# Experts loop of a hybrid decoder step: transpose of the first activation half placed before the last up grain, first tail down block placed after the first down grain, some lo splits placed later

## What is computed

```python
gu   = xs @ w_gu[e] + b_gu[e]                  # 1024 -> 2048
gate = minimum(gu[:, :1024], 7.0)
up   = clip(gu[:, 1024:], -7.0, 7.0)
act  = gate * sigmoid(1.702 * gate) * (up + 1.0)
out  = (act @ w_down[e] + b_down[e]) * prob    # 1024 -> 1024
y    = segment_sum(out, token)
```

## Time and profile before

| | us |
|---|---|
| median of 3 runs (lowest, highest) | 2195.52 (2192.89, 2197.51) |
| profiled execution, span | 2192.6 |
| PE busy in it | 2059.1 (94%) |
| DVE busy | 1621.2 (74%) |
| ACT busy | 1279.9 (58%) |
| POOL busy | 784.6 (36%) |
| start of the first item, end of the last | 665.90, about 2142.7 |

### The profile page before, as it was taken

The page is one execution under the profiler, slowest core; times in us unless marked ns, Lnnn a source line. Parts: engine busy times, 40 slices in busy tenths (PEclk is TensorE's granted clock), DMA queues, the critical chain, the costliest instruction groups (busy, mean ns, idle before and its releaser), DMA issues.

```text
span 2192.6 us, 38702 instructions
## 1 busy us (share of the span) xinstructions
PE 2059.1 (94%) x11946; PEld 1503.0 (69%) x11947; DVE 1621.2 (74%) x2213; ACT 1279.9 (58%) x1717; POOL 784.6 (36%) x997
## 2 busy tenths in 40 slices
PE   6998999999958999999999999999999999999995
PEld 4996766666647676676666677767676676777552
DVE  4533456666668687787777689988897798899667
ACT  3632443334316676676765568767776676877544
POOL 3224345555623233223331323433232233334124
PEclk7999999999969999999999999999999999999997
DMA  9767511211268787898887789999898898999665
GB/s 343 232 222 267 170 49 51 68 49 54 87 229 330 264 316 281 293 351 289 278 310 255 260 294 375 364 341 331 290 370 324 287 339 333 345 359 390 243 226 180
DMA packets 154530, 572.25 MB, mean 261 GB/s; under 512 B 22560, under 2 KB 41773, under 8 KB 120165
## 3 DMA queue, kind: packets, MB, share of 16 engines
q1 hardware_dynamic: 127405, 511.87, 62.1%
q0 software_dynamic: 25520, 56.53, 10.6%
q10 hardware_dynamic: 1552, 3.13, 0.4%
HBM read 521.36 MB, written 50.29 MB: 261 GB/s over the span
## 4 chain that ended last, share of the span: by engine, by line
PE 53%; DVE 6%; issue 6%; ACT 4%; DVEq 1%; DMA 0%; ACTq 0%; POOLq 0%
PE pg L2235 9%; PE pg L2236 9%; PE pg L2238 9%; PE py L2194 6%; PE py L2170 4%; PE py L2171 4%; PE py L2174 4%; PE pg L2208 3%; DVE lo L2459 3%; ACT hi L2371 2%; PE pt L2165 1%; PE pg L2228 1%; DVE pair L2477 1%; DVE pair L2473 1%; ACT sigm L2379 1%
## 5 line engine op out<-in xcount | busy, mean ns | idle before, releaser
L2235 PE MATMUL pg<-hi,xs 128*128 128x512 f32 x1056 | 429.4, 407 | 0.0
L2236 PE MATMUL pg<-lo,xs 128*128 128x512 f32 x1056 | 411.8, 390 | 0.0
L2459 DVE TENSOR_TENSOR lo<-spare,hi 128x1024 fp32r<-128x1024 f32 x264 | 306.3, 1221 | 85.2 <-ACT hi L2371 82.2
L2459 DVE TENSOR_TENSOR lo<-w_out,hi 128x1024 fp32r<-128x1024 f32 x272 | 312.4, 1220 | 59.2 <-ACT hi L2371 59.1
L2238 PE MATMUL pg<-hi,xs 128*128 128x512 f32 x1056 | 325.5, 389 | 0.0
L2459 DVE TENSOR_TENSOR lo<-raw,hi 128x1024 fp32r<-128x1024 f32 x264 | 314.1, 1220 | 7.1
L2371 ACT ACTIVATE hi<-spare 128x1024 fp32r<-128x1024 f32 x264 | 260.2, 1050 | 43.7 <-PE pg L2238 43.7
L2371 ACT ACTIVATE hi<-raw 128x1024 fp32r<-128x1024 f32 x264 | 271.0, 1053 | 25.1 <-PE pg L2238 24.2
L2371 ACT ACTIVATE hi<-w_out 128x1024 fp32r<-128x1024 f32 x272 | 265.5, 1050 | 32.4 <-SPq L2002 28.0
L2235 PEld LDWEIGHTS pg<-hi,xs 128*128 128x128 f32 x1056 | 198.3, 188 | 72.7 <-DVE lo L2459 13.3
L2170 PE MATMUL py<-hi,aT 128*128 128x512 f32 x528 | 218.8, 414 | 12.1 <-ACT aT L2383 5.5
(11 more groups left out here) (487 smaller groups left out, 3646.2 us busy)
## 6 DMA issues: line engine op xcount, KB each, us to landing
w_out<-in_w_gu SPq DMA_DIRECT2D x136, 1024.0 KB, 6.9
spare<-in_w_gu SPq DMA_DIRECT2D x132, 1024.0 KB, 10.3
raw<-in_w_down SPq DMA_DIRECT2D x132, 1024.0 KB
ada_w<-in_w_ada SPq DMA_DIRECT2D x4, 2048.0 KB
spare<-in_w_ada SPq DMA_DIRECT2D x4, 2048.0 KB
moe_rows<-small SPq DMA_DIRECT2D x9, 512.0 KB, 6.7
w_v<-in_w_in SPq DMA_DIRECT2D x2, 2048.0 KB, 17.4
w_i<-in_w_in SPq DMA_DIRECT2D x2, 2048.0 KB, 18.6
```

The lines of the kernel that those rows point to most:

```text
L2235: pe.matmul(pg[u][b][:, :], xs[:, kt, 0, :], wh[:, u, :], start=False, stop=False)
L2236: pe.matmul(pg[u][b][:, :], xs[:, kt, 0, :], wl[:, u, :], start=False, stop=False)
L2459: dve.tensor_tensor(lo[q % RING][:, :, :], grain(q % GRAINS), hi[q % RING][:, :, :].bitcast(F32), ALU.subtract).then_inc(s["lo"], 1)
```

## The change

On PE, `transpose_act(i, 0)` moves from behind up grain 15 to in front of it. `down_tail(i, 0, tail)` moves from in front of down grain 0 to behind it. On DVE, the order of the lo splits around the two activations is another: `head` ends with grain 17, not 18; splits 18 and 19 stand behind `swiglu(i, 0)`; split 20 stands between `rows_lo` of half 0 and `act_lo` of half 1; split 21 between `act_lo` of half 1 and `rows_lo` of half 1; splits 22 and 23 behind that, and `select` last. No instruction is added or removed, and the orders of ACT, SP and POOL are as they were.

```diff
@@ tensor engine, item(i, tail)
                 for q in range(HEAD, GU):
+                    if q == GU - 1:
+                        transpose_act(i, 0)
                     if tail and q in TAILED:
                         pe.wait_ge(s["lo"], i * GRAINS + q + 1)
...
                     up_grain(i, q)
 
-                transpose_act(i, 0)
                 if tail:
                     tail_act(i, tail)
                 transpose_rows(i + 1, 0)
...
-                    if tail and kt == 0:
+                    if tail and kt == 1:
                         pe.wait_ge(s["aT_t"], i + 1)
                         down_tail(i, 0, tail)
                     down_grain(i, kt)
@@ vector engine
             def head(i):
-                for q in range(RING, GU + 3):
+                for q in range(RING, GU + 2):
                     split_lo(i, q)
...
             def foot(i):
                 swiglu(i, 0)
-                for q in range(GU + 3, GU + 5):
+                for q in range(GU + 2, GU + 4):
                     split_lo(i, q)
                 act_lo(i, 0)
                 swiglu(i, 1)
                 rows_lo(i + 1, 0)
+                split_lo(i, GU + 4)
+                act_lo(i, 1)
                 split_lo(i, GU + 5)
-                split_lo(i, GU + 6)
-                act_lo(i, 1)
                 rows_lo(i + 1, 1)
+                for q in range(GU + 6, GU + 8):
+                    split_lo(i, q)
                 select(i + 1)
-                split_lo(i, GU + 7)
                 for q in range(RING):
                     split_lo(i, GRAINS + q)
```

## The result

The changed kernel is slower. It takes 2271.7 us in the median of four runs (2270.82 to 2272.34), the kernel before 2194.2 us (2192.3 to 2197.51): ratio 1.0357, 95% interval 1.0345 to 1.037. The forecast was 2170, with 2165 to 2181 as range.

What follows compares the result with a forecast made beforehand. PE, busy 94%, and a nearly even DVE in items without tails bound the kernel. Gains of 7.2, 10.3, 8.2 and 0 make 25.7 us; 2195.5 less that gives 2169.8, range 2165 to 2181.

Steps and rivals of the forecast that it cites:

- the term for the back-to-back items: Eight items without a tail behind another such: DVE loses idle times of 0.67 and 0.26 us, 0.9 gained each, 7.2 total.
- The rival on the other side: DVE's unbroken splits delay POOL's copy of the row weights by 2.5 us in 17 items: 2213 us, chance 0.04.
- The early transpose: Half 0's transpose on PE, ahead of up grain 15: same 0.44 us cost, waits 1.5 us at most behind tails.
- The tail's first block: The tail's down block on PE, behind down grain 0: net 0.68 us gained per item with a tail of 32.
- Tail of 64: Four items: the early transpose's wait of 0.63 and 0.1 for switches take back 0.78; nothing, within 0.2 us.
- DVE's two checks: In DVE's new order, half 1's lo part and the next rows' second half keep 0.4 and 0.3 us to spare.
- The period of 35.9 set by DVE: Back-to-back items without a tail: DVE's own work of 35.9 us is the floor of their length.
- The sum: Gains over all items without a tail and with tails of 32 and 64: 25.7 us off in all.
- 8.86: Time in us from the start of the first activation on DVE to the transpose of half 1 on PE.
- DMA as the floor: Weights can't come faster in back-to-back items, so their 7.2 us gain goes: 2177 us, chance 0.07.
- DVE's new waits: Both reserves in DVE's order fail, DVE stands about 0.6 us in each of 17 items: 2180 us, chance 0.12.
- No effect: Something unseen sets the period and the change doesn't reach the bound: 2195 us stays, chance 0.04.

Runs made afterwards that it cites:

- e3: The changed kernel plus one DVE clamp of about 0.6 us, its only input in PSUM, ahead of the split of grain 8: 2228.6 us, ratio 1.0164.
- e4: The changed kernel plus one DVE subtraction of about 0.6 us, two inputs in SBUF, ahead of the split of grain 8: 2279.3 us, ratio 1.0396.
- e5: The changed kernel, with DVE waiting once for its own last split ahead of the split of grain 8, no instruction added: 2168.4 us, ratio 0.9876.
- e7: The changed kernel plus a small DVE instruction reading 32 columns of PSUM ahead of each of splits 8, 10 and 12: 2171.9 us, ratio 0.9895.
- e9: The changed kernel with one DVE wait ahead of split 8, and half 0's transpose left behind grain 15 for tails of 64: 2166.2 us, ratio 0.9869.
- e6_small_psum: The changed kernel plus one small DVE instruction reading 32 columns of PSUM ahead of the split of grain 8: 2219.3 us, ratio 1.0113.

## Why the prediction was wrong

**The step that failed** is the term for the back-to-back items, 8 x 0.9 = 7.2, and in it the sentence "I take that DVE loses both its idle times". DVE did lose the 0.67 us, but the prediction put nothing against it, with "SP's and POOL's lists are untouched" as its ground. That idle time was not waste: it was the opening through which POOL's scatter and gather got their turn. In 8 items its loss cost 11.8 us each where 0.9 was to be gained. `e3` against `e4` shows that DVE's kind of instruction decides, `e5` and `e7` that the opening takes back the whole of the loss. Not all of the 11.8 is time held off: in the mean of the eight the scatter's instruction ends 12.3 us later in the item than before, its landing takes 5.1 us longer, and 6 us had been to spare.

**The rival on the other side** was the right mechanism at the wrong instruction. It named DVE's unbroken splits, POOL and the missing 0.67, with 0.04 as its chance and 2213 as its time. But it looked at the copy of `now`, which is indeed held off and indeed harmless, and not at the scatter ahead of it in POOL's list. Its price of 2.5 us in 17 items stood on no row; the runs show 11.8 in 8. The scatter was held off in the same item already (4.40 us, where one that gets through at once takes 1.6 to 1.75), and what it delays is the rest of DVE's run and then a landing of 10 us. I never asked of each POOL instruction what it would do if DVE had no gap, though DVE's run without a gap was itself part of the forecast.

**Point by point, most of the rest held.** The early transpose costs nothing by itself and waits behind tails, 1.25 us (1.5 at the most had been forecast); the item is 37.72 all the same. The tail's first block: an item with a tail of 32 got 0.58 shorter (49.08 to 48.50); 0.68 had been counted. Tail of 64: 0.06 longer, forecast as nothing; the early transpose waits there as forecast, and `e9` takes it back. DVE's two checks held: PE doesn't wait before down grain 6, apart from the stall late in the first two items, which the kernel before had as well (3.6 and 2.9 us; now 3.7 and 4.8). The period of 35.9 set by DVE: 35.8 in `e5`. The sum: 25.7 us off; `e5_self_wait`, the same change with an opening, is 26.4 us below its kernel before (ratio 0.9876), and 24.4 in the repeat. But that agreement is in part luck. In the profiled executions, `e5` gains 22.5 us within the loop, and another 2.8 because its first item starts earlier, where the change does nothing. The items without a tail give 17.8 (17.5 forecast), those with a tail of 32 only 4.9 (8.2 forecast): 6.4 from eleven of them, less 1.5 that the first one loses. Two small sums of the prediction are off by what nothing hangs on: the parts given for 8.86 (2.88, 2.3, 0.6, 3.0) add up to 8.78, and 1388.07 with 2 x 1.39 is 1390.85, not 1390.87. As it was run, the change missed the forecast by 2271.7 - 2169.8 = 102 us.

**The other rivals.** DMA as the floor: refuted, the DMA engines move 389 GB/s in `e5` and items still shrink. DVE's new waits: they don't bite, the back-to-back items last 35.8 in `e5`. No effect: refuted by all runs.

## What to carry to other kernels

Before you count an engine's idle time as gain, ask who uses the gap: here a small pause of VectorE is what lets GpSimd's gathers and scatters go on, and on an engine that is made gapless the pause must be put back on purpose, at 0.1 to 0.2 us, and close ahead of what it is to let through. A long duration of an instruction that should be short (4.40 us against 1.75) is a sign of a wait that no semaphore shows, and it deserves the same question as an idle time: what ended it. When two engines wait for each other's progress, as DVE for the scatter's landing and the scatter for DVE's pause, a saving of 1 us can tip into a loss of 12.

## What the runs showed of the hardware

A GpSimd scatter (its DMA instruction, which runs on POOL for some 1.7 us when nothing holds it) can be held off by VectorE's subtractions with two SBUF inputs, when these follow each other without idle time: 16.64 us in the changed kernel, 17.24 in `e4_sbuf_op`. In both it ends 1.55 us behind the end of that run. A VectorE instruction of 0.69 us with its input in PSUM lets it through, so does one with 32 columns, and so does 0.12 us without any instruction. In these traces it also goes by how far VectorE's last idle time lies back: up to the sixth instruction behind it, 452 of 452 GpSimd instructions got through within 2.07 us (the scatter of 1.72 us at 1514.77 is one), later 3 of 178.

The Trainium skill, SBUF — State Buffer, section "Who interferes with whom", says that a VectorE instruction with two SBUF inputs contends with a GpSimd instruction that reads SBUF, and that one with at most one SBUF input, outside the 2-port perf modes, doesn't. The held-off scatter and the PSUM instruction that frees it agree with that. The same section says of `tensor_tensor` that it wasn't seen to stall DMAs issued from GpSimd, with the reason marked as inferred. There the measurements differ: 16.64 us, though not close behind an idle time of VectorE.

The count also fits what the gather does: it gets through between two splits in `e5_self_wait` (begun at 1361.06, ended at 1362.58) and in the kernel before (1371.16 to 1373.23), but not in `e3_psum_op` (1368.09 to 1379.08) and `e6_small_psum`, where it begins about as soon behind the opening. In the first two the opening was a time without an instruction. In the others it was an instruction, which let one GpSimd instruction through, and VectorE had had no idle time since long before. Left open is why an idle time lets more than one through, and whether the number of instructions behind it counts or the time (the line lies some 6.8 to 7.5 us behind it): no run was made to tell them apart.
